# Seven-product pairs for columns 0 and 1 of three down projections, their sums on GpSimd, and one square root moved, in a float32 two-block transformer kernel

## The reference, cut to what matters

```python
h = rms_norm(x, g_pre_ffn)                       # (256, 2048); block 1 also scales and shifts it
f = (silu(h @ w_gate) * (h @ w_up)) @ w_down     # 2048 -> 5632 -> 2048
x = x + rms_norm(f, g_post_ffn)                  # block 1 multiplies the norm by a gate gt2
```

## Time and profile before

| | |
|---|---|
| median of 3 runs | 2517.43 us (2516.72 to 2517.58) |
| the profiled execution | 2518.82 us, of which the span of the profile is 2517.0 us |
| TensorE busy | 2484.9 us, 99% |
| VectorE busy | 2105.2 us, 84% |
| ScalarE busy | 1373.6 us, 55% |
| GpSimd busy | 3.9 us |
| mean granted TensorE clock | 0.997 |

### The profile page before, as it was taken

One profiled execution on the slowest core, in us unless ns is written; L12 is line 12 of the kernel. 1 busy time (PEld: TensorE's weight loads), 2 busy tenths in 40 slices (PEclk: granted clock), 3 DMA queues, 4 the chain that ended last, 5 costly groups with the idle time before them and its releaser, 6 DMA issues.

```text
span 2517.0 us, 30496 instructions
## 1 busy us (share of the span) xinstructions
PE 2484.9 (99%) x11234; PEld 2036.8 (81%) x11234; DVE 2105.2 (84%) x2695; ACT 1373.6 (55%) x1886; POOL 3.9 (0%) x11
## 2 busy tenths in 40 slices
PE   7999999999999999999999999999999999999998
PEld 6788877788878888888888888888888888888887
DVE  8999999999889999778997777666689986689977
ACT  4445778764565554455554545554565554455544
POOL 0000000000000000000000000000000000000000
PEclk9999999999999999999999999999999999999999
DMA  9998666888955556965555554445555555555563
GB/s 384 355 350 325 228 212 228 286 289 315 360 192 213 201 201 218 363 258 197 196 218 199 191 201 168 167 170 202 197 187 186 215 199 184 198 203 188 189 247 112
DMA packets 80791, 578.26 MB, mean 230 GB/s; under 512 B 9166, under 2 KB 9462, under 8 KB 10881
## 3 DMA queue, kind: packets, MB, share of 16 engines
q1 hardware_dynamic: 79056, 567.25, 61.4%
q10 hardware_dynamic: 1074, 6.37, 0.7%
q0 software_dynamic: 512, 2.69, 0.3%
HBM read 574.15 MB, written 3.70 MB: 230 GB/s over the span
## 4 chain that ended last, share of the span: by engine, by line
PE 88%; DVE 5%; ACT 2%; issue 2%; DMA 2%; DVEq 0%; ACTq 0%; SPq 0%
PE bank L975 76%; PE bank L948 9%; DVE wlo L1921 2%; DMA raw<-in_w_in 2%; DVE raw L1931 1%; DVE cv L2157 1%; ACT whi L1300 1%; PE bank L879 1%; ACT PR L1300 1%; DVE cv L1912 0%; ACT SS L1516 0%; PE bank L1177 0%; DVE PART L2004 0%; PE bank L1220 0%; PE bank L1092 0%
## 5 line engine op out<-in xcount | busy, mean ns | idle before, releaser
L1921 DVE TENSOR_TENSOR wlo<-raw,whi 128x1024 fp32r<-128x1024 f32 x819 | 991.1, 1222 | 252.6 <-ACT whi L1300 245.5
L1300 ACT ACTIVATE whi<-raw 128x1024 fp32r<-128x1024 f32 x819 | 853.4, 1056 | 621.1 <-PE bank L975 400.4
L975 PE MATMUL bank<-whi,HTh 128*128 128x512 f32 x2216 | 605.7, 395 | 7.8 <-ACT HTh L1300 4.6
L975 PE MATMUL bank<-wlo,HTh 128*128 128x512 f32 x2216 | 595.0, 390 | 1.5 <-DVE wlo L1921 1.5
L975 PE MATMUL bank<-whi,HTl 128*128 128x512 f32 x2216 | 594.9, 390 | 0.0
L975 PEld LDWEIGHTS bank<-wlo,HTh 128*128 128x128 f32 x2216 | 416.1, 188 | 90.5 <-DVE wlo L1921 3.4
L975 PEld LDWEIGHTS bank<-whi,HTl 128*128 128x128 f32 x2216 | 416.6, 188 | 89.1
L975 PEld LDWEIGHTS bank<-whi,HTh 128*128 128x128 f32 x2216 | 409.6, 188 | 97.2 <-issue 9.0
L1931 DVE CUSTOM_DVE_ANT_0 raw<-raw,GT,VECS 128x2048 f32<-128x2048 f32 x95 | 222.8, 2347 | 1.8 <-DMA raw<-in_w_ada 1.5
L975 PE MATMUL bank<-whi,ACTh 128*128 128x512 f32 x656 | 176.7, 389 | 0.0
L975 PE MATMUL bank<-wlo,ACTh 128*128 128x512 f32 x656 | 176.7, 389 | 0.0
(11 more groups left out here) (314 smaller groups left out, 2063.4 us busy)
## 6 DMA issues: line engine op xcount, KB each, us to landing
raw<-in_w_in SPq DMA_DIRECT2D x126, 1024.0 KB, 4.9
raw<-in_w_ada SPq DMA_DIRECT2D x95, 1024.0 KB, 6.6
raw<-in_w_down SPq DMA_DIRECT2D x76, 1024.0 KB, 4.9
raw<-in_w_up SPq DMA_DIRECT2D x71, 1024.0 KB, 4.8
raw<-in_w_gate SPq DMA_DIRECT2D x65, 1024.0 KB, 5.1
raw<-in_w_o SPq DMA_DIRECT2D x16, 1024.0 KB, 7.1
raw<-in_w_out SPq DMA_DIRECT2D x16, 1024.0 KB, 4.8
GT<-in_w_down SPq DMA_DIRECT2D x12, 1024.0 KB, 4.8
```

The source lines that it names most:

```text
L975: i = e.matmul(bank[2 * ch.st + t][:, :], (xl if ps == 1 else xh)[:, k, tk(t)], (lo if ps == 2 else hi)[:, j * 512:j * 512 + 512], start=c ...
L1300: return e.activation(dst, src, ACT.Copy, scale=scale)
L1921: e.tensor_tensor(lo, src, r32(hi), S_).then_inc(lo_done, 1)
```

## The change

Three things are changed. First, columns 0 and 1 of down01, down10 and down11 become a seven-product pair too, by the new lists DOWN3 (down01, down11) and DOWN0 (down10). The sums are made once for a stage and serve both its pairs. Second, the ten additions of the sums of these three stages go from VectorE's list to GpSimd's; their high part stays on ScalarE and their low part on VectorE (`low_sums`), both now at slot 6 of the stage (before: slot 15 or 17 for the high part, and 11 or 12 for the start on VectorE). Third, at the seam in front of ffn00 ScalarE takes `mroot0` before the eviction of the last column's second half, not behind it.

```diff
+DOWN0 = ["g"] * 7 + [1, "g", 5, "g", 6, "g", 7, 2, "u", 4, "u", 3] + ["u"] * 8
+DOWN3 = ["g"] * 5 + [1, "g", 5, "g", 6, "g", 7, 2, "u", 4, "u", 3] + ["u"] * 6
...
-            order = {(1, 0, 2): DOWN1, (0, 1, 2): DOWN2, (1, 1, 2): DOWN2}.get((layer, part, j // 2 * 2))
+            order = {(1, 0, 0): DOWN0, (0, 1, 0): DOWN3, (1, 1, 0): DOWN3, (1, 0, 2): DOWN1, (0, 1, 2): DOWN2, (1, 1, 2): DOWN2}.get((layer, part, j // 2 * 2))
...
 def forms_high(site):
-            w.wait_ge(*s_dve[site]("j"))
+            w.wait_ge(*(s_dve if site[0] == "f" else s_pool)[site]("j"))
...
             if n == 0:
+                root(0, rr_mod[:, 0:1], res_dve[0]("quad0"), "mroot0")
                 evict(aparts[0], (1,))
-                root(0, rr_mod[:, 0:1], res_dve[0]("quad0"), "mroot0")
                 res_root(0, 1)
...
-            lane.begin(M[f"down{n}1"] + 15, forms_high(("d", n, 1)))
+            lane.begin(M[f"down{n}1"] + 6, forms_high(("d", n, 1)))
...
-        lane.begin(M["down10"] + 17, forms_high(("d", 1, 0)))
+        lane.begin(M["down10"] + 6, forms_high(("d", 1, 0)))
...
+        def low_sums(site):
+            w.wait_ge(*s_act[site]("hi"))
+            e.tensor_tensor(SLs[site][:, :, :], S32s[site][:, :, :], r32(SHs[site][:, :, :]), S_).then_inc(*s_dve[site].one("lo"))
+            yield 1
...
-            lane.begin(M[f"down{n}1"] + 11, forms_left(("d", n, 1)))
-        lane.begin(M["down10"] + 12, forms_left(("d", 1, 0)))
+            lane.begin(M[f"down{n}1"] + 6, low_sums(("d", n, 1)))
+        lane.begin(M["down10"] + 6, low_sums(("d", 1, 0)))
...
     def gpsimd(e):
...
+        def forms_left(n, part):
+            site, q = ("d", n, part), 4 * STAR
...
+            w.wait_ge(*f_act[n](part, STAR))
+            w.wait_ge(*f_dve[n](part, STAR))
+            if part:
+                w.wait_ge(pe_done, M[f"down{n}1"])
+            else:
+                w.wait_ge(*upm[n](0, 5, 1))
...
+                if after:
+                    w.wait_ge(*d(after))
+                e.tensor_tensor(out, a, b, op).then_inc(*d.one(name))
...
         w.wait_ge(scr_in, 16)
+        forms_left(0, 1)
         w.wait_ge(pe_done, B1)
...
+        forms_left(1, 0)
+        forms_left(1, 1)
```

More of the change, by code:

```diff
@@ L283, in plan_ffn @@
                     chs = [p.chunk("down", (layer, part, j + i), f"a{layer}{part}", "DVE", apart=part == 1 and j + i == 3,
-                                   st=None if part else j + i) for i in range(2)]
+                                   st=j + i if part == 0 else 2 + i if layer and j == 0 else None) for i in range(2)]
                     p.duo(chs, [("w_down" + ext, (j + i) * 11 + f0 // 4) for i in range(2)], fn // 4, order, ("d", layer, part))
@@ L579, in build @@
     s_act = {i: steps("s_act_" + "".join(map(str, i)), ["hi"]) for i in SITES}
-    s_dve = {i: steps("s_dve_" + "".join(map(str, i)), [*"abcdefghij", "lo"]) for i in SITES}
+    s_dve = {i: steps("s_dve_" + "".join(map(str, i)), [*("abcdefghij" if i[0] == "f" else ""), "lo"]) for i in SITES}
+    s_pool = {i: steps("s_pool_" + "".join(map(str, i)), list("abcdefghij")) for i in SITES if i[0] == "d"}
     held = {i: steps("held_" + "".join(map(str, i)), [(pc.chunk.j, HELD[pc.form]) for pc in P.pieces
@@ L2347, in forms_left @@
             q = 4 * STAR
-            xh, xl = XS["f%d" % n if site[0] == "f" else "a%d%d" % site[1:]]
+            xh, xl = XS["f%d" % n]
             (h00, l00), (h01, l01), (h10, l10), (h11, l11) = [
@@ L2352, in forms_left @@
             d = s_dve[site]
[L2353 to L2364, removed]
+            w.wait_ge(*res_dve[2 * n](3, 1))
+            w.wait_ge(*rows_of(2 * n, 3, 1))
+            w.wait_ge(*(g_dve[2](7) if n else m_dve("lo", 6)))
+            w.wait_ge(*part_act[2 * n](7))
             for name, out, a, b, op, after in (
@@ L2375, in forms_left @@
             w.wait_ge(*s_act[site]("hi"))
-            if site[0] == "f":
-                w.wait_ge(*res_act[2](3, 1) if n else part_act[0](15))
+            w.wait_ge(*res_act[2](3, 1) if n else part_act[0](15))
             e.tensor_tensor(SLs[site][:, :, :], S32s[site][:, :, :], r32(SHs[site][:, :, :]), S_).then_inc(*d.one("lo"))
@@ L2673, in gpsimd @@
         w = Waits(e)
+        plus, minus = ALU.add, ALU.subtract
+        def forms_left(n, part):
+            site, q = ("d", n, part), 4 * STAR
+            xh, xl = XS["a%d%d" % (n, part)]
+            (h00, l00), (h01, l01), (h10, l10), (h11, l11) = [
+                [r32(x[:, q + 2 * h:q + 2 * h + 2, tk(t)]) for x in (xh, xl)] for t in R(2) for h in R(2)]
+            s1, s2, s3, s4 = [tri(S32s[site][:, i, :], 2) for i in R(4)]
+            d = s_pool[site]
+            w.wait_ge(*f_act[n](part, STAR))
[4 more added lines that the diff above has]
+                w.wait_ge(*upm[n](0, 5, 1))
+            for name, out, a, b, op, after in (
+                    ("a", s1, h10, h11, plus, None), ("b", s3, h00, h10, minus, None), ("c", s1, s1, l10, plus, "a"),
+                    ("d", s3, s3, l00, plus, "b"), ("e", s1, s1, l11, plus, "c"), ("f", s3, s3, l10, minus, "d"),
+                    ("g", s2, s1, h00, minus, "e"), ("h", s2, s2, l00, minus, "g"), ("i", s4, h01, s2, minus, "h"),
+                    ("j", s4, s4, l01, plus, "i")):
+                if after:
+                    w.wait_ge(*d(after))
+                e.tensor_tensor(out, a, b, op).then_inc(*d.one(name))
         e.memset(ident[:, :], 0.0).then_inc(*pro_pool.one("zero"))
```

## The result

The changed kernel took 2531.53 us (median of 4 runs, 2528.27 to 2532.68), the one before beside it 2517.51 us (4 runs, 2516.72 to 2518.21): 1.0053 times as long, 95% interval 1.004 to 1.0066, 14.0 us more. The profiled execution was the fastest of the four, 2528.27 us with a span of 2526.4 us, that is 9.4 us above the span before.

The account below looks back on a forecast made before the run. TensorE, busy 99%, was taken to bound the kernel, with VectorE overfull at the stages' starts; -4.1 - 0.7 + 9.8 + 3.2 + 3.0 = +11.2 us on 2517.43 gave 2528.6 us, range 2522 to 2535.

Parts of the forecast that it names:

- The matmuls, -4.1 us: In down01, down10 and down11 eight half-products become seven: 6 matmuls, 1.36 us less in each stage.
- The root, -0.7 us: At the seam the chain behind the earlier root gains 0.7 us; bounds 0 and -1.7, another -1.4 if the clock doesn't fall.
- The waits, +9.8 us: TensorE at form 5 waits for VectorE's low part of the sums, 4.8 us in down01 and 5.0 in down11.
- No wait in down10: Form 5 of down10 has the sums' low part ready with 2.2 us to spare, so the stage keeps its gain.
- GpSimd's hold, +3 us: GpSimd's additions hold up VectorE by 1.5 us a stage, on top of both waits; covered in down10.
- rival 1: VectorE and GpSimd shut each other out at the stages' starts, 3 us a stage; 2532 us, chance 0.17.
- GpSimd's addition, 0.9 us: One of GpSimd's ten additions a stage takes 0.9 us, between 0.42 and 1.4; not on the path up to 1.7.
- rival 3: GpSimd itself is late with the sums, at 2.4 us an addition; +24 us, 2541 us, chance 0.07.
- The clock, +3.2 us: Slow matmuls at half clock after the waits in down01 and down11 cost 1.6 us each, between 0 and 2.3.
- rival 2: Half a loss: the clock doesn't fall and GpSimd costs VectorE nothing; +5.0 us, 2522.4 us, chance 0.14.
- Nothing pays this back: No later TensorE idle time in down01 and down11 could shrink; behind the wait VectorE has 5 us of lead again.
- rival 4: Form 5 does not wait, so the gain stands alone; -4.8 us, 2512.6 us, chance 0.06.

Follow-up runs that it names:

- root_down10: Kernel before with the moved root and the new pair in down10 alone, its ten additions on GpSimd: 2516.03 us, ratio 0.9993.
- light_vector: Changed kernel with GpSimd's additions as zero fills, no weight differences in down01 and down11, sums' high and low parts at slots 3 and 4: 2514.3 us.
- root_only: Kernel before with only the root moved ahead of the eviction at the seam: 2516.61 us, ratio 0.9995.
- pairs_no_root: Changed kernel with the root put back to its old place: 2532.34 us, ratio 1.0057.
- memsets: Changed kernel with GpSimd's thirty additions replaced by fills with zeros, which read nothing: 2528.1 us, ratio 1.0039.
- sums_on_vector: Changed kernel with the ten additions of down01 and down11 back on VectorE in slots 1 to 5: 2535.61 us, ratio 1.0072.
- the second trace: Profile of the changed kernel run again, unchanged: 2531.36 us, ratio 1.0053, span 2530.0 us.
- low_early: Changed kernel with the sums' high part at slot 3 and low part at slot 4 in down01 and down11: 2527.02 us, ratio 1.0037.

## Why the prediction was right

The forecast was 2528.6 us, range 2522 to 2535, slower; measured were 2531.53 us and 2531.36 us. The profiled execution came within 0.4 us of the forecast (2528.27), but by luck: its prologue was 1.8 us shorter than before, and its slow stretches lay well. Step by step:

- **The matmuls, -4.1 us.** Right: down10, where nothing waits, is 1.36 us shorter to the hundredth, in the changed kernel and in `root_down10`. In down01 and down11 the gain shows only in `light_vector`, and there less what VectorE still holds back: 0.88 and 0.72 us.
- **The root, -0.7 us.** Near. The stage behind the seam began 0.94 us earlier in the trace, by the step that was given (the sum's accumulator bounds it: the reduction still waits 1.66 us for ScalarE). In all the seam is 1.7 us shorter in this trace and in `root_only`, where the clock doesn't fall. It is 0.5 us shorter in `pairs_no_root`, where the clock doesn't fall either and the root is not moved, and 1.2 us in `root_down10`, where the root is moved and the clock falls as before. So the root is worth 1.1 to 1.2 us and the clock some 0.5, not the 1.4 of my far end. The runs give 1.0 us, which they can't tell from nothing.
- **The waits, +9.8 us.** The place, the releaser and VectorE's unbroken work are as forecast. With fills, and so without GpSimd's hold, they measure 4.73 and 4.91 us (`memsets`), where the rows added up to 4.8 and 5.0.
- **No wait in down10.** Right: the low part was ready 21.1 us after the stage's start (forecast 20.9), form 5 came at 23.1.
- **GpSimd's hold, +3 us.** Right in size: the waits are 1.7 and 1.5 us longer than with fills, where 1.5 a stage was taken. My reason, that transposes would fill most of the time, was wrong for down01: of the 10.1 us of additions transposes fill 3.2 (1316.28 to 1318.10, 1319.64 to 1321.03). They are indeed untouched, and the engines otherwise shut each other out as rival 1 had it. That the size came out is in part luck. VectorE's own instructions became 2.1 us longer in down01 (0.79 for the two products, 0.54 and 0.25 for the low parts, 0.53 for the small one); 0.45 of it falls ahead of a transpose that TensorE makes, so TensorE is later by as much and the wait grows by the rest. By rival 1 the price was 3 us a stage for five such holds; it was 2.1, of which 1.7 us reached the wait. The trace agrees with the rule of the Trainium skill (SBUF — State Buffer, section Who interferes with whom) that rival 1 names: GpSimd's addition at 1318.61 took 1.61 us while the low part of 1318.13 ran to its end at 1319.61, and the low part of 1313.97 took 1.76 us beside additions, and 1.22 us in `memsets`.
- **GpSimd's addition, 0.9 us.** 0.74 us beside transposes, up to 1.77 beside VectorE, 10.1 us for ten. Not on the path, which ends rival 3. The estimate from the Trainium skill (GPSIMD Engine Reference, section Performance versus the Vector engine), 0.6 us, is low by a fifth.
- **The clock, +3.2 us.** Mis-sized, and the main term that was: the loss was 1.5 + 1.5 us in the first trace, 2.75 + 2.17 in the second, 2.77 + 2.14 in `pairs_no_root`, 2.29 + 2.56 in `sums_on_vector`. In the first three the waits are the same, and the stretch lies otherwise to them. Around 2.4 us each would have been the better value, and the largest passed my bound of 2.3, since I bounded the stretch by the 4.7 us of a window in the earlier trace rows. It is 6.8 us long here (10.2 in `sums_on_vector`), and the trace before already had one of 6.8 us, which windows set to its ends show:

```profile
17.80:20.90 3.10, 0.02 (x1) 0.00 (x0) 2.96 (x5) 0.60 (x1) 0.00 (x0) 1.00 1.01 423
21.00:27.80 6.80, 5.34 (x13) 4.21 (x14) 6.14 (x9) 2.56 (x4) 0.00 (x0) 0.50 1.01 422
```

So the 0.93 of the earlier trace rows, from which rival 2 took its support, was a mean over a clock at 1.00 until 20.9 and at 0.50 behind.
- **Left out:** 0.45 us at the start of down01, through the transpose above; 0.16 us at each wait, since the idle time is counted from the modelled end of the last matmul. With the clock at 4.9 the sum is -4.1 - 1.0 + 12.8 + 4.9 + 0.5 + 0.3 = +13.4, against 13.0 for the span of the second trace and 14.0 for the medians. It is 2.2 us more than forecast: 1.7 from the clock, 0.8 left out, 0.3 back from the root; waits and hold together (12.8) are as forecast.
- **"Nothing pays this back ... Behind the wait VectorE has 5 us of lead".** Right for the kernel as it stands. But it hid that the opening of the stage is overfull, which `low_early` brought out: at piece 8 and at the held results the next three waits stand in line.

Rival 1 was right about what the two engines do to each other. Its time, 2532 us, is close to the medians too, but its extra 3.8 us are not what came: most of the excess is the clock's. Rival 2 fell (the clock did fall), rival 4 too. Not tried: a version that takes the joins or the last activations' transposes to another engine, and forms later in the list of down01 and down11; the runs don't say whether these would keep the gain.

## What to carry to other kernels

Before work is put into the opening of a stage, add up what the second engine has to do there until the first new deadline, instruction by instruction, and not by its share of the span: here 84% busy on average hid a stretch in which it had no pause, and 2.7 us of matmuls saved in two stages cost 12.8 us of waiting. When a wait shows one late instruction, ask what stands next in line: here moving it forward turned one wait of 6.4 us into four of 5.6 us in all, of which 1.3 at the old place. And count a wait of several us on TensorE at its length plus a loss for the clock behind it: here 1.5 to 2.8 us for each wait of 4.7 to 8.5 us.

## What the runs showed of the hardware

- VectorE with two operands in SBUF and GpSimd's additions lengthen each other: a low part of 128x1024 took 1.76 and 1.48 us instead of 1.22, an instruction of only 128x16 took 0.70 instead of 0.17, an addition on GpSimd 1.2 to 1.8 instead of 0.74. Transposes on VectorE (one operand) took the same time beside them, and so did two products that read one of their operands from PSUM (`SNP <- bank, SNP`, 1.29 us). Fills on GpSimd left the two products `SG` at 1.28 us, which took 2.07 beside additions.
- For the same wait of 6.4 us the half-speed stretch began 2.7 us after TensorE stopped in one execution and 5.1 us after in another. At the seam a wait of 2.35 us was followed by half speed in `root_down10` and by full speed in `root_only`, which have the same program up to there; on this stretch, where TensorE has idle times, half speed over 3.4 us cost 0.5 us.
